# Token blocks of 64 instead of 32 in the expert stage of a hybrid encoder layer, with half-row biases and x tiles normed one by one

## The reference

```
x = x + concat(attention(norm(x)), state_space(norm(x))) @ w_out
h = norm(x)
logits = h @ w_router + b_router              # 32 experts
top_val, top_idx = top_k(logits, 4)           # each token goes to 4 experts
w = softmax(top_val)
for each expert e, for the tokens that chose it:
    g = min(h @ w_gate[e] + b_gate[e], 7);  u = clip(h @ w_up[e] + b_up[e], -7, 7)
    act = g * sigmoid(1.702 g) * (u + 1)
    x[token] += w * (act @ w_down[e] + b_down[e])
```

## Time and profile before

| | us |
|---|---|
| median of 3 runs | 1425.62 (1425.61 to 1426.26) |
| the profiled execution's own time | 1427.83 |
| its span | 1425.9 |
| granted clock of PE, mean | 0.97 |

### The profile page before, as it was taken

One profiled execution on the slowest core, in us unless ns is written; L12 is line 12 of the kernel. 1 busy time (PEld: TensorE's weight loads), 2 busy tenths in 40 slices (PEclk: granted clock), 3 DMA queues, 4 the chain that ended last, 5 costly groups with the idle time before them and its releaser, 6 DMA issues.

```text
span 1425.9 us, 40195 instructions
## 1 busy us (share of the span) xinstructions
PE 1320.1 (93%) x18053; PEld 811.5 (57%) x18053; DVE 449.6 (32%) x1049; ACT 218.1 (15%) x487; POOL 191.3 (13%) x142
## 2 busy tenths in 40 slices
PE   5999989998699999999998988998998998999984
PEld 3466677665456666666555554664665654666651
DVE  3643577554322222223221221221221322222210
ACT  2123244331011111100110000110110001001110
POOL 0000220000101121111111211121121121012111
PEclk9999999998699999999999999999999999999995
DMA  9000330005999999999999999999999999999993
GB/s 349 4 1 0 123 132 1 30 30 221 389 362 372 391 393 388 396 382 400 394 395 403 398 412 397 407 406 391 411 402 397 408 398 410 388 411 386 403 408 126
DMA packets 79360, 446.18 MB, mean 313 GB/s; under 512 B 13227, under 2 KB 21491, under 8 KB 30035
## 3 DMA queue, kind: packets, MB, share of 16 engines
q1 hardware_dynamic: 63922, 425.85, 74.2%
q0 software_dynamic: 15120, 17.20, 5.7%
q10 hardware_dynamic: 144, 0.52, 0.1%
HBM read 433.30 MB, written 14.94 MB: 314 GB/s over the span
## 4 chain that ended last, share of the span: by engine, by line
PE 48%; SPq 40%; DMA 7%; issue 2%; DVE 2%; POOL 1%; ACT 0%; POOLq 0%; DVEq 0%; ACTq 0%
SPq L609 39%; PE pair L1832 24%; PE pair L1580 7%; PE pair L1564 4%; DMA ring<-in_w_down 2%; DMA rest<-in_w_gate 2%; PE pair L1541 2%; PE pair L1732 2%; PE pair L1672 2%; DMA ring<-in_w_in 1%; PE pair L1791 1%; PE pair L1694 1%; POOL ring L712 1%; PE pair L1804 1%; DMA rest<-normed_rows,rest 1%
## 5 line engine op out<-in xcount | busy, mean ns | idle before, releaser
L1832 PE MATMUL pair<-ring,rest 128*32 128x256 f32 x14832 | 847.0, 383 | 43.9 <-DMA ring<-in_w_down 21.3
L1832 PEld LDWEIGHTS pair<-ring,rest 128*32 128x32 f32 x14832 | 477.9, 110 | 358.4 <-DMA ring<-in_w_down 31.3
L752 POOL DMA_INDIRECT out<-rest x82 | 128.2, 1564 | 769.7 <-ACT rest L995 716.0
L1038 DVE TENSOR_TENSOR rest<-pair,rest 128x512 f32<-128x512 f32 (+4 forms) x113 | 88.9, 786 | 434.7 <-PE pair L1832 419.4
L995 ACT ACTIVATE rest<-rest 128x256 f32<-128x256 f32 x82 | 36.5, 500 | 535.2 <-DVE rest L1038 535.2
L1580 PE MATMUL pair<-ring 128*128 128x512 f32 (+1 forms) x256 | 100.7, 552 | 1.7 <-DVE ring L1038 1.1
L1580 PEld LDWEIGHTS pair<-ring 128*128 128x128 f32 x256 | 49.2, 194 | 48.9 <-issue 45.3
L1038 DVE TENSOR_TENSOR rest<-rest 128x512 f32<-128x512 f32 (+7 forms) x98 | 62.8, 650 | 35.0 <-ACT rest L977 26.2
L977 ACT ACTIVATE rest<-rest 128x512 f32<-128x512 f32 (+3 forms) x34 | 24.4, 718 | 304.5 <-DVE rest L1367 300.8
L1334 DVE TENSOR_SCALAR rest<-pair 64x1 int32<-64x1 f32 (+3 forms) x34 | 5.2, 152 | 183.5 <-issue 179.6
L1832 PE MATMUL pair<-rest 128*32 128x256 f32 x912 | 57.3, 390 | 5.6 <-DMA rest<-in_w_down 3.4
(11 more groups left out here) (177 smaller groups left out, 875.7 us busy)
## 6 DMA issues: line engine op xcount, KB each, us to landing
ring<-in_w_up SPq DMA_DIRECT2D x121, 1024.0 KB
ring<-in_w_gate SPq DMA_DIRECT2D x120, 1024.0 KB
ring<-in_w_down SPq DMA_DIRECT2D x120, 1024.0 KB
rest<-in_w_gate SPq DMA_DIRECT2D x8, 1024.0 KB
rest<-in_w_down SPq DMA_DIRECT2D x8, 1024.0 KB
rest<-in_w_up SPq DMA_DIRECT2D x7, 1024.0 KB
ring<-in_w_in SPq DMA_DIRECT2D x1, 4160.0 KB, 15.4
ring<-in_x SPq DMA_DIRECT2D x8, 512.0 KB, 6.0
```

The lines of the kernel that those rows point to most:

```text
L752: p.indirect_dma_start(out=out_rows, out_offset=bass.IndirectOffsetOnAxis(ap=sidx[vi.ring][:, g:g + 1].bitcast(I32), axis=0), in_=yrow_b[v ...
L1038: return v.tensor_tensor(out=out, in0=a, in1=b, op=op)
L1832: last = T.matmul(ps[q * TOK:(q + 1) * TOK, g * QW:(g + 1) * QW], x, pieces[slot][:, kk, q * QW:(q + 1) * QW], start=(k == 0 and g % 2 == ...
```

## The change

The first part is in the expert stage. `blocks(g)` takes the blocks of a visit in twos: a pair of 64 tokens, and where g is odd, one block of 32 at the end. A pair uses a stationary slice of 128 x 64 and two matmuls with half of the weight's columns each (512), into partitions 0 to 63 and 64 to 127. It lies in PSUM as 128 rows (half, token) by 512 columns. Its output rows are 2 KB, and one indirect DMA adds a pair. The single block at the end of an odd visit stays as it was. The second part follows from it: biases are kept in half rows of 512, three shuffles of 512 columns for a position into one buffer `bias_h`, and a single block's bias is added in two steps with masks for even and odd quarters. The third part is in the front: inverse norms are computed tile by tile, the six parameter DMAs are issued by ACT, the first weights come in eight DMAs (one per k), and the first four channels are computed with k outside and the channel inside, before `dt`.

```diff
+def blocks(g):
+    return [(2 * b, 2) for b in range(g // 2)] + [(g - 1, 1)] * (g % 2)
...
-            sp.dma_start(const, d["const"]).then_inc(s_const, 16)
+            sp.dma_start(const, d["const"][:, 0:C_END]).then_inc(s_const, 16)
...
-            for name, r0, n in (("norm_mix", 0, 8), ("conv_b", 8, 8), ("conv_w", 16, 40),
...
-                sp.dma_start(praw[r0:r0 + n, :], src).then_inc(s_par, 16)
-            for n, (a, b) in enumerate(((XBC0, INW), (0, Z0), (Z0, XBC0))):
-                sp.dma_start(w_in[:, :, a:b], w_in_d[:, :, a:b]).then_inc(s_win[n], 16)
+            for n, (a, b) in enumerate(((XBC0, INW), (0, Z0), (Z0, XBC0))):
+                if n == 0:
+                    for k in range(KT):
+                        sp.dma_start(w_in[:, k, a:b], w_in_d[:, k, a:b]).then_inc(s_wx[k], 16)
+                else:
+                    sp.dma_start(w_in[:, :, a:b], w_in_d[:, :, a:b]).then_inc(s_win[n], 16)
...
+                    sp.dma_start(rep2, d["const"][:, C_REP2:C_ALL]).then_inc(s_rep2, 16)
...
-                for g in range(vi.G):
+                for n, (g, width) in enumerate(blocks(vi.G)):
                     p.indirect_dma_start(
-                        out=out_rows, out_offset=bass.IndirectOffsetOnAxis(ap=sidx[vi.ring][:, g:g + 1].bitcast(I32), axis=0),
-                        in_=yrow_b[vi.b][:, g * QW:(g + 1) * QW], in_offset=None, bounds_check=SEQ * NQ - 1, oob_is_err=False,
-                        compute_op=ALU.add).then_inc(s_scat, 16)
+                        out=out_rows[width],
+                        out_offset=bass.IndirectOffsetOnAxis(ap=sidx[vi.ring][:, n:n + 1].bitcast(I32), axis=0),
+                        in_=yrow_b[vi.b][:, g * QW:(g + width) * QW], in_offset=None,
+                        bounds_check=SEQ * NQ // width - 1, oob_is_err=False, compute_op=ALU.add).then_inc(s_scat, 16)
...
                 link(nc.scalar.activation(junkx, xsb[:, t, :], ACT.Square, accum_out=ssq[:, t:t + 1]))
-            rms(rstd, ssq, DM).then_inc(s_rstd, 1)
+                rms(rstd[:, t:t + 1], ssq[:, t:t + 1], DM).then_inc(s_rstd, 1)
...
+                if vi.G % 2:
+                    o = slice(w, w + QW)
+                    lk(v.scalar_tensor_tensor(out=dst[:, o], in0=bias[:, 0:QW], scalar=even_c, in1=ps[:, o], op0=ALU.mult,
+                                              op1=ALU.add))
+                    ins = v.scalar_tensor_tensor(out=dst[:, o], in0=bias[:, QW:HALF], scalar=odd_c, in1=dst[:, o],
+                                                 op0=ALU.mult, op1=ALU.add)
+                if both:
+                    ins = tt(cut(dst[:, 0:w], both, HALF), cut(ps[:, 0:w], both, HALF), times(bias, both), ALU.add)
...
+            four = [(ch, begin(f"xb{ch}")) for ch in CHANNELS[:4]]
+            for k in range(KT):
+                pe.wait_ge(s_wx[k], 16)
+                for ch, ps in four:
+                    last = conv_product(ps, ch, k)
+                    if k == KT - 1:
+                        end(last, f"xb{ch}")
...
-                        for g in range(vi.G):
-                            x = xT[:, k, g * TOK:(g + 1) * TOK] if m < 2 else aT[:, g, k % 2, k // 2, :]
-                            for q in range(NQ):
-                                last = T.matmul(ps[q * TOK:(q + 1) * TOK, g * QW:(g + 1) * QW], x,
-                                                pieces[slot][:, kk, q * QW:(q + 1) * QW],
-                                                start=(k == 0 and g % 2 == 0), stop=(k == KT - 1), skip_group_check=True)
+                        for g, width in blocks(vi.G):
+                            size, w, cols = width * TOK, width * QW, NQ // width
...
+                            for q in range(cols):
+                                last = T.matmul(ps[q * size:(q + 1) * size, g * QW:g * QW + w], x,
+                                                pieces[slot][:, kk, q * w:(q + 1) * w],
+                                                start=(k == 0), stop=(k == KT - 1), skip_group_check=True)
```

More of the change, by code:

```diff
@@ L164 @@
 C_END = C_SIN + NT * HD
+C_REP2 = C_END
+C_ALL = C_REP2 + P
+HALF = DM // 2
+def blocks(g):
+    return [(2 * b, 2) for b in range(g // 2)] + [(g - 1, 1)] * (g % 2)
+GM_AT = {g: C_GM + sum(len(blocks(n)) for n in range(1, g)) for g in range(1, MAX_GROUPS + 1)}
 def constants():
@@ L186, in constants @@
     c[:, C_REP:C_GM] = t % TOK == q % TOK
-    c[:, C_GM:C_EPS] = t // TOK == np.arange(MAX_GROUPS)[None, :]
+    for g, at in GM_AT.items():
+        for n, (first, width) in enumerate(blocks(g)):
+            c[:, at + n] = row // (width * TOK) == first // width
+    c[:, C_REP2:C_ALL] = t % (2 * TOK) == q % (2 * TOK)
+    c[:, C_H2] = 2 * FAR + row // (2 * TOK)
+    c[:, C_HB] = row // (2 * TOK)
+    c[:, C_EVEN] = row // TOK % 2 == 0
+    c[:, C_ODD] = row // TOK % 2 == 1
     c[:, C_EPS] = EPS
@@ L481, in hybrid_layer @@
         at_piece = {u: divmod(n, NRING) for n, u in enumerate(STREAM)}
-        scattered = [sum(VISITS[w][1] for w in range(v)) for v in range(NV + 1)]
+        scattered = [sum(len(blocks(VISITS[w][1])) for w in range(v)) for v in range(NV + 1)]
         def visit(v):
@@ L1349, in places @@
-                v.tensor_copy(wv[vi.ring][:, 0:vi.G], ps[:, :, 1]).then_inc(s_tfree[use[1]], 1)
-            def by_group(ap, vi):
-                return cut(ap[:, 0:vi.G * QW], vi.G, QW)
-            def plus_bias(vi, dst, m):
+                for first, last, parts, row in ((0, both, 2, h2_c), (both, n, NQ, q4_c)):
+                    if first < last:
+                        v.tensor_scalar(out=sidx[vi.ring][:, first:last].bitcast(I32), in0=ps[:, first:last, 0],
+                                        scalar1=float(parts), scalar2=row, op0=ALU.mult, op1=ALU.add)
@@ L1775, in replicate @@
                 c = vi.G * TOK
-                turned(T.matmul(ps[:, 0:2 * vi.G], rep_c[0:c, :],
-                                dmask[vi.b][0:c, 0:vi.G, :].rearrange("p a b -> p (a b)"), start=True, stop=True), use)
+                n, both = len(blocks(vi.G)), vi.G // 2
+                for first, last, lay in ((0, both, rep2), (both, n, rep_c)):
+                    if first < last:
+                        ins = T.matmul(ps[:, 2 * first:2 * last], lay[0:c, :],
+                                       dmask[vi.b][0:c, first:last, :].rearrange("p a b -> p (a b)"), start=True, stop=True)
+                turned(ins, use)
             def kp_rows(ap, blocks):
```

177 lines of the change are left out of this document (107 added, 70 removed).

## The result

The changed kernel takes 1432.03 us (median of 6 runs, 1430.74 to 1433.15); the kernel before took 1425.59 beside it. The ratio is 1.0051, 95% interval 1.0040 to 1.0063, so it is slower by some 6.4 us. The forecast was 1421.9. The profiled execution took 1433.15 us where 1424.1 was worked out.

The account below looks back on a forecast made before the run. PE was taken to bound the kernel ahead of the expert stage, PE and DMA both full in it, DMA setting the end from position 14. -3.1 - 1.1 + 0.5 = -3.7 from 1427.83: 1424.1, median 1421.9; own range 1417 to 1426, wide 1409 to 1443.

Parts of the forecast that it names:

- scatter row of 2 KB: Adding scatters of pairs: 172 ns a row, twice a plain row's 86, with bounds of 137 and 206 ns.
- a pair against two blocks of 32: PE's products: half the matmuls, each twice as long, 0.86 against 0.864 us; 34 pairs x 24 make -4 us.
- start of position 14: End of the first expert stretch: 812.25 - 7.0 + 39.2 = 844.4 us before the front's gain, 32 us later.
- pieces ready there: Weight ring at position 14: full again with 14 pieces instead of 3.6, since the DMA waits for PE.
- one piece afterwards: Weight transfers from position 14 on: 2.773 x 0.9925 = 2.752 us for each of 206 remaining pieces.
- The front: Ahead of the expert stage: PE starts at 18.2 to 18.3 instead of 21.35 us, -3.1, bounds 0 and -4.
- I take 0.20: Three-block positions: two changes of form in each k cost 0.20 us, 43 us in all, 39 after the pairs' 4.
- third rival: Three-block positions: a pair of changes costs 0.34 us, PE has 69 us more, sum 1452; chance 0.21 (anywhere from 1428 to 1452).
- The waits: First expert stretch, up to position 14: PE's 7.0 us of waiting for weights go.
- Stock and pace: Weight ring and transfers: PE's extra 39 us paid nearly whole from stock; last weight at 1411.3 instead of 1412.4, -1.1 us.
- DVE and the biases: Expert stage: shuffles +1.0 us a position, beside PE; only the last product's second bias step is on the path, +0.5.
- the 7.8 us of DMA time: Scatters with 2 KB rows: 44.9 instead of 52.7 us of all engines, bounds -16 and 0, counting only where DMA sets the pace.

Follow-up runs that it names:

- by_piece: The changed kernel with one loop turned, so each ring piece does the pair's products of both k first, halving the changes of form: 1411.30 us, 0.9925 of before.
- by_piece_swap: by_piece with positions 3 and 4 exchanged, everything behind them as it was: 1419.09 us, ratio 0.9951 against the kernel before.
- snake: by_piece with the block order also reversed in every other ring piece, a quarter of the changed kernel's changes of form: 1412.97 us, 0.9924 of before.
- front_only: The kernel before with only the front part of the change, its expert stage left as it was: 1420.65 us, ratio 0.9977.
- blocks_only: The kernel before with only the expert-stage part of the change, its front left as it was: 1434.33 us, ratio 1.0079.

## Why the prediction was wrong, step by step

| step | predicted | measured |
|---|---|---|
| PE starts the channels | 18.2 | 17.32 |
| first product earlier by | 3.1 | 2.9 |
| scatter row of 2 KB | 172 ns | 176 to 178 ns |
| a pair against two blocks of 32 | 0.86 us, no gain | the same |
| two changes of form | 0.20 us | 0.27 to 0.29 us |
| start of position 14 | 841.3 | 857.5 |
| pieces ready there | 14 | 13.4 |
| one piece afterwards | 2.752 us | 2.716 us |
| last weight | 1408.2 | 1418.7 |
| from there to the end | 15.9 | 14.5 |

(The start of position 14 is the prediction's 844.4 less the 3.1 us of the front, and so the last weight.)

**The front** was right in place and nearly in size. The parameters' transpose no longer holds DVE, and DVE ends at 17.0 us where 18.2 was worked out. PE was 4.0 us earlier at the channels and 4.8 us (360.0 for 364.8) at the wait for the first gather, and lost 1.9 there: it waited 9.8 us, before 7.9. The timelines, before and after:
```profile
372.68 1.52 PE L1791 MATMUL pair<-rest 96*128 96x96 f32 x8 [7.86 <-DMA rest<-normed_rows,rest]
```
```profile
369.79 1.53 PE L1863 MATMUL pair<-rest 96*128 96x96 f32 x8 [9.78 <-DMA rest<-normed_rows,rest]
```

**The step that failed** is "I take 0.20" for the two changes of form in a k. The prediction had bounded the price at 0.14 to 0.34 from remainders in the chain and argued that part of each remainder was not the change. It is 0.286. Over the nine positions, up to the start of position 14, starts of products give about 55 us instead of the 39 summed: 16 us. (The prediction counted all 216 k there; the down product of position 13, eight of them, comes behind that start.) The measured 0.286 is well past the 0.217 that the prediction named as the point from which its third rival decides and short of the 0.34 for which that rival was priced at 1452: it is this rival that came true, in part, and through it alone the measured 1432.0 lies in the stated 1409 to 1443. The prediction's own sum with 0.286 would be 0.086 x 216 = 18.6 us more, 1440.5; what brings it down to 1432 are the waits and the pace below, so the rest of the sum was off too, by terms that partly cancel. The Trainium skill (TensorEngine Tiling (Array Packing), Key Properties) says that a change of tiling mode drains TensorE; the 0.27 to 0.29 us for each pair of changes, in three kernels with different numbers of them, agree with it, though no record shows a drain as such.

**The step that was missing** is the clock at the first product. The prediction took PE's rate after the gather for granted. The low clock lasted 11.3 us instead of 3.8, and the starts of positions 1 and 3 come 5 us later than the changes of form explain. Some 1.6 of these 5 belong to a second stretch of low clock near 411 us (0.83 in 410 to 420, where the kernel before has 1.00), behind a wait of 1.81 us for DVE (L1434); before, the same wait is 1.38 us. The Trainium skill (TensorE: Matmul & The Clock Gate, HAM oscillation — how this bites in real kernels) says that waits between groups of matmuls bring the low level back. The rows agree so far as the clock was at 0.50 in such waits and full again in all six kernels with the added matmuls, though it had fallen some 10 us ahead of the longest one, in a stretch where PE was busy about half of the time. Why the changed kernel gets its clock back later than the one before, from gaps of about the same length, is not settled. by_piece and by_piece_swap, with the same work up to there, came out on different sides in most of their runs.

**The waits.** The 7 us of waiting for weights that were to vanish were about 12, by the same comparison of starts (the rows of before list 7.0 us in waits long enough to be named). So 841.3 + 16 + 5 - 5 = 857, the measured 857.5.

**Stock and pace.** The mechanism held. The ring was full to 13.4 pieces at position 14, and PE's extra time was largely paid from it: PE reached that place 45 us later than before, and the last weight landed 6.3 us later. The pace was better than forecast by 0.036 us a piece, 7.4 us over 206.6 pieces. The prediction also had PE waiting for weights from position 14 on; in fact PE is busy for 351.34 of 352.50 us up to 1210, while the transfers run at a share of 1.02. A piece took 2.1% less than in the kernel before, where the scatter rows alone would make 0.75%. What makes up the rest was not tested, and the rows' own part was measured in snake only. Part of it is the third stretch, whose share is 0.99 where it was 0.96.

Together: 10.5 us at the last weight, less 1.4 in the tail, are the 9.0 us between 1424.1 and 1433.15.

**DVE and the biases** cost next to nothing, as costed: the changed kernel's DVE is busy for 141 of 486 us in the first stretch, PE's one wait for it there is 0.4 us longer than before, and by_piece, with the same DVE work, is 1.3% shorter by the ratios.

## What to carry to other kernels

Where two forms of matmul alternate in an inner loop, count the changes and not only the matmuls: the loop order that groups them by form (here within a ring piece) cost nothing and turned +0.5% into -0.75%. Before a saving on the transfers is counted, ask which engine empties the buffer; the 7.8 us of DMA time worked out here could only be paid from position 14 on, and PE's extra time outweighed it. A gap in front of the stage that sets the pace is worth a look at the granted clock, and a few unused matmuls in it are a cheap test.

## What the runs showed that was not expected

- One round trip between a matmul form of 64 columns and one of 32 cost 0.27 to 0.29 us, whatever their number in a product (8, 4 or 2).
- An adding scatter row took about 100 ns with 1 KB (103 by the earlier trace rows) and 176 to 178 ns with 2 KB; plain rows of 2 KB had taken 86 ns.
- The granted clock stayed at its lower level for 2.6 us (front_only) to 16 us (blocks_only) after the first product had started, and 14 records of unused matmuls in the gap had it back before the product in all six kernels that have them (1.00 from 370 us on). By the medians this was worth 1.4 us in before, 6.6 in after and 9.9 in by_piece_swap. In the two that gained most the DMA share had fallen to 0.73 and 0.67 in the window from 380 us on; in before it was 1.02.
